# Prompt tokens in groups of 256, 384 and 384, the later ones beside the expert gathers

## The reference

```
xn = rmsnorm(x);  q_lat(384), kv_lat(256), k_rope(32), pool_in(512), gates(2x1024) = xn @ w_in
q = rope(rmsnorm(q_lat) @ w_q_up), 8 heads of 64+32;  c = rmsnorm(kv_lat);  k = [c @ w_uk, rope(k_rope)];  v = c @ w_uv
q and k are RMS-normed per head; prompt: causal softmax over 1024 keys
sample: softmax over 8 x 32 cached pages of 128 tokens (found through page_table) and the 8 new ones
pool: trailing means over 2, 4, 8, 16 tokens minus the token, a linear layer per group
h = x + (sigmoid(g1) * (attn @ w_attn_br) + sigmoid(g2) * (pool @ w_pool_br)) @ w_out
PEER: s = rmsnorm(h) @ w_q scored against 2 x 128 keys, 8 heads; top 16 of each half, top 16 of the 256 sums
      expert ids -> y = h + sum over 8 x 16 experts of softmax gate * gelu(xn2 . u[id]) * v[id]
```

## Time and profile before

| what | value |
|---|---|
| median of 3 runs | 4643.17 us (4634.75 to 4645.33) |
| the profiled execution | 4673.63 us |
| its span, first to last instruction | 4671.8 us |
| mean granted TensorE clock | 0.849 |
| bytes read from and written to HBM | 1275 MB and 29 MB |

### The profile page before, as it was taken

How to read it: one execution, slowest core, us unless ns; L and a number is a source line. 1 busy time by engine, 2 the same in 40 slices (tenths; PEclk the granted TensorE clock), 3 DMA queues, 4 the chain that set the end, 5 groups by cost and what they waited for, 6 DMA issues and landing times.

```text
span 4671.8 us, 47213 instructions
## 1 busy us (share of the span) xinstructions
PE 3692.4 (79%) x13481; PEld 1607.9 (34%) x13481; DVE 2738.3 (59%) x6886; ACT 998.0 (21%) x2045; POOL 2470.3 (53%) x2234
## 2 busy tenths in 40 slices
PE   8998787999998577777877778777878767676556
PEld 4433565444454233333333333333333323230001
DVE  3334331001104878878888888887878765666643
ACT  1121332001200224223323323322322310200000
POOL 0001100000000777777777777777777776677776
PEclk9998878999999788888888888888887878777778
DMA  2002002111323999999999999999999999999999
GB/s 105 1 28 36 2 0 95 41 40 59 109 63 101 361 388 381 396 380 388 396 394 388 388 399 396 392 396 386 396 396 389 374 405 412 386 407 390 372 372 382
DMA packets 441801, 1306.94 MB, mean 280 GB/s; under 512 B 90218, under 2 KB 146923, under 8 KB 438707
## 3 DMA queue, kind: packets, MB, share of 16 engines
q0 software_dynamic: 313344, 1140.99, 62.6%
q1 hardware_dynamic: 128242, 163.51, 10.7%
HBM read 1275.49 MB, written 28.75 MB: 279 GB/s over the span
## 4 chain that ended last, share of the span: by engine, by line
POOL 28%; DMA 14%; PE 11%; issue 10%; DVE 3%; SPq 2%; ACT 1%; DVEq 0%; ACTq 0%; POOLq 0%
POOL arena L1280 28%; DMA arena<-in_peer_v,arena 9%; PE ps_m L1343 4%; PE ps_m L1591 3%; DMA arena<-in_cache_krope 2%; DMA arena<-key_scores 1%; SPq L1544 1%; DMA arena<-in_peer_u,arena 1%; DVE arena L1385 1%; PE ps_m L1581 1%; PE ps_m L1616 1%; PE ps_m L1599 1%; SPq L1542 1%; PE ps_m L1600 1%; PE ps_m L1932 0%
## 5 line engine op out<-in xcount | busy, mean ns | idle before, releaser
L1343 PE MATMUL ps_m<-arena 128*32 128x512 f32 x4352 | 1171.3, 742 | 584.0 <-DMA arena<-in_peer_v,arena 558.3
L1385 DVE CUSTOM_DVE_ANT_0 arena<-arena 128x1024 f32<-128x1024 f32 x1088 | 1318.6, 1225 | 523.1 <-DMA arena<-in_peer_u,arena 491.5
L1280 POOL DMA_INDIRECT arena<-in_peer_u,arena x1088 | 1207.9, 1110 | 639.6 <-issue 329.0
L1280 POOL DMA_INDIRECT arena<-in_peer_v,arena x1088 | 1200.4, 1103 | 403.3 <-issue 306.9
L1343 PEld LDWEIGHTS ps_m<-arena 128*32 128x32 f32 x4352 | 193.8, 120 | 1346.2 <-DMA arena<-in_peer_v,arena 921.5
L1591 PE MATMUL ps_m<-arena 128*128 128x512 f32 x1056 | 567.7, 664 | 2.6 <-ACT arena L1671 2.4
L1581 PE MATMUL ps_m<-const,arena 128*128 128x128 f32 x528 | 135.7, 346 | 177.7 <-DMA arena<-in_cache_krope 148.8
L1591 PEld LDWEIGHTS ps_m<-arena 128*128 128x128 f32 x1056 | 202.5, 213 | 196.9 <-issue 190.5
L1671 ACT ACTIVATE arena<-ps_m 128x512 f32<-128x512 f32 x264 | 158.2, 599 | 514.5 <-PE ps_m L1591 510.0
L944 POOL COPY arena<-arena 128x1024 f32 (+1 forms) x8 | 8.3, 1042 | 489.4 <-POOLq L821 407.4
L1663 ACT ACTIVATE arena<-ps_m 128x256 f32<-128x256 f32 x264 | 101.4, 384 | 689.7 <-PE ps_m L1582 688.7
(11 more groups left out here) (235 smaller groups left out, 4465.4 us busy)
## 6 DMA issues: line engine op xcount, KB each, us to landing
arena<-in_cache_ckv SPq DMA_DIRECT2D x256, 128.0 KB
arena<-in_w_merge SPq DMA_DIRECT2D x16, 1536.0 KB, 9.2
arena<-in_w_peer SPq DMA_DIRECT2D x32, 576.0 KB, 4.1
arena<-in_peer_u,arena POOLq DMA_INDIRECT x1088, 7.6
arena<-in_peer_v,arena POOLq DMA_INDIRECT x1088, 7.6
arena<-key_scores SPq DMA_DIRECT2D x68, 128.0 KB, 10.8
key_scores<-arena SPq DMA_DIRECT2D x32, 256.0 KB, 4.5
arena<-in_w_front SPq DMA_DIRECT2D x1, 4864.0 KB, 18.9
```

The lines of the kernel that those rows point to most:

```text
L1280: self.nc.gpsimd.indirect_dma_start(out=ring[:, slot, :], out_offset=None, in_=self.I[table], in_offset=bass.IndirectOffsetOnAxis(ap=self. ...
L1343: mm = self.nc.tensor.matmul(self.acc[32 * j:32 * j + 32, n, :], self.diag[:, (q0 + j) // 16 % DIAGS, (q0 + j) % 16, :], self.v_ring[:, (q ...
L1385: self.nc.vector.tensor_tensor_reduce(out=u, in0=u, in1=self.xrep[jg % self.XBUF], scale=1.0, scalar=0.0, op0=ALU.mult, op1=ALU.add, accum ...
```

## The change

The front half no longer exists as such. A class `Prompt` with the same arithmetic works on a group of prompt tokens, and there are three: tiles 0 and 1 with the 64 sample tokens (320 columns), tiles 2 to 4, tiles 5 to 7 (384 each). The first is emitted at once on every engine, ahead of the gathers; its first units are routed and its first rows replicated by DMA. The two others are written into the slots of the expert program: `Plan` lays their pieces one behind the other, each with an estimated length in us divided by a rate (2.65 and 2.4 us a slot result), and `paced` raises the rate until the scores are ready before their routing. They take slots 0 to 198 and 199 to 441. The 64 page groups follow at slot 442 with six slots each instead of twelve (842 is their end), the sample's merge, output and scores from 852, four slots a step instead of six.

What comes with it: front, query, merge, output and score weights are loaded once per group, in rings of two or three buffers; keys and values of a group are stored to DRAM and read back with those of the groups before; heads are projected as pairs (128 columns) and the rotary parts as quads; the window sums and the multiply by the norm are on DVE, no longer on POOL; the sigmoid is written as a tanh of the half; the cached latent and rope rows are one tensor, one load a page instead of two; the barrier between the halves is gone.

The diff, cut to its core:

```diff
-PAGES_AT, PAGE_SLOTS = 16, 12
-SAMPLE_AT = PAGES_AT + DB * (NPAGES // GP * PAGE_SLOTS + 2) + 12
+PAGE_SLOTS = 6
...
+GROUPS_OF = (2, 3, 3)
...
+        groups, tile, base = [], 0, None
+        for i, tiles in enumerate(GROUPS_OF):
+            groups.append(paced(i, tile, tiles, base))
+            base, tile = groups[-1].done_at + (2 if i else 0), tile + tiles
+        assert ex.end + GROUP_WORDS <= HALO, (ex.end, HALO)
+        pr = Prompt(env, ex.end, ex.spare, sem, ps, rt, ex, groups)
+        pg = Pages(env, ex.end, sem, ps, base + 8)
...
+            pr.sync(Now(sp), groups[0], groups[1])
+            main = Main("SP", sp, ex.sync(sp))
+            for g, following in zip(groups[1:], after[1:]):
+                pr.sync(main, g, following)
+            pg.sync(main)
+            sm.sync(main)
+            main.finish()
...
+            main = Main("POOL", pool, ex.pool(pool))
+            pg.clear(main, pr)
+            main.finish()
...
+            pr.tensor(Now(pe), groups[0])
+            main = Main("PE", pe, ex.tensor(pe))
+            for g in groups[1:]:
+                pr.tensor(main, g)
+            pg.tensor(main)
+            sm.tensor(main)
+            main.finish()
...
+def route_slot(unit):
+    return TOPK * (unit - 5) + 4
+def paced(i, tile, tiles, base):
+    if base is None:
+        return Group(i, tile, tiles, None, 1.0)
+    rate, unit = 2.4, H * tile
+    while True:
+        g = Group(i, tile, tiles, base, rate)
+        if g.half_at <= route_slot(unit) and g.done_at <= route_slot(unit + 4):
+            return g
+        rate += 0.05
+        assert rate < 20
...
+class Now:
+    def __init__(self, eng):
+        self.eng = eng
+    def to(self, slot):
+        return self.eng
...
+class Plan:
+    def __init__(self, base, rate):
+        self.base, self.t, self.rate, self.begin, self.end = base, base, rate, {}, {}
+    def piece(self, name, us, lead=0):
+        if self.base is None:
+            return
+        self.t += lead
+        self.begin[name] = self.t
+        self.t += us / self.rate
+        self.end[name] = self.t
+    def at(self, name, part=0.0):
+        if self.base is None:
+            return 0
+        return int(self.begin[name] + part * (self.end[name] - self.begin[name]))
...
+class Group:
+    def __init__(self, i, tile0, tiles, base, rate):
+        self.i, self.tile0, self.tiles, self.base = i, tile0, tiles, base
+        self.T, self.first, self.last = tiles * P, i == 0, tile0 + tiles == PT
+        self.N = self.T + (NS if self.first else 0)
+        self.col0 = tile0 * P
+        self.units = [(h, t) for h in range(H) for t in range(tiles)]
+        self.unit0 = H * tile0
+        mm, p = 0.9 * self.N / 512, Plan(base, rate)
+        mt = 0.9 * self.T / 512
+        self.p = p
+        p.piece("sum_x", 8 * mm, 1)
+        for j in range(11):
+            if j == 4:
+                p.piece("sum_q", 3 * mm)
+            if j == 7:
+                p.piece("sum_kv", 2 * mm)
+            p.piece(f"chunk{j}", 8 * mm, 2 if j == 0 else 0)
+        for u in range(6):
+            p.piece(f"q{u}", (4 if u < 4 else 7) * mm, 1 if u == 5 else 0)
+        p.piece("pick_q", mm)
+        for t in range(tiles):
+            p.piece(f"v{t}", 1.8)
+        for s in range(6):
+            p.piece(f"sq{s}", mm, 0.4 if s >= 2 else 0)
+        for u in range(4):
+            p.piece(f"k{u}", 3 * mm, 0.3 if u >= 2 else 0)
+        p.piece("pick_k", 2 * mm, 0.5)
+        for c in range(G):
+            p.piece(f"lin{c}", mm)
+        for s in range(6):
+            p.piece(f"sk{s}", mm, 1 if s == 0 else 0.2 if s >= 2 else 0)
+        for u, (h, t) in enumerate(self.units):
+            n = tile0 + t + 1
+            p.piece(f"a{u}", n * 0.6 + 0.2, 4 if u == 0 else 0)
+        p.piece("a_end", 0.5, 0.5)
+        for t in range(tiles):
+            p.piece(f"at{t}", 1.1, 0.7 if t == 0 else 0)
+        for d in range(KD):
+            p.piece(f"gate{d}", 16 * mt, 1 if d == 0 else 0)
+            p.piece(f"branch{d}", 8 * mt)
+        for k in range(KD):
+            p.piece(f"out{k}", 2 * tiles * 0.9, 1 if k == 0 else 0)
+        for t in range(tiles):
+            p.piece(f"tp{t}", 2.1, 2 if t == 0 else 0.5)
+        for j in range(2 * H):
+            p.piece(f"s{j}", 8 * mt + tiles * 0.25, 0.7 if j == 0 else 0)
+        p.piece("s_end", tiles * 0.25, 0.5)
...
+        self.half_at = 0 if base is None else p.after("s8", 1)
+        self.done_at = 0 if base is None else p.after("s_end", 3)
...
+        for h in range(2, H):
+            u = (h - 1) * g.tiles
+            sp = main.to(g.after(f"a{max(u - 3, 0)}"))
+            sp.wait_ge(self.s_done, g.unit0 + u)
+            self.load_key(sp, g, h)
```

More of the change, by code:

```diff
@@ L123, in build @@
[L123 to L133, removed]
@@ L137 @@
[L137 to L147, removed]
-LATT = ATS - 2 * H * NS
-LATE = LATT - 2 * N_IDS
-QT = TOP - H * TOK
-KT = QT - H * TOK
-CT = KT - 2 * TOK
@@ new lines, in _ @@
+            pr.vector(Now(dve), groups[0])
+            main = Main("DVE", dve, ex.vector(dve))
+            for g in groups[1:]:
+                pr.vector(main, g)
+            pg.vector(main)
+            sm.vector(main)
+            main.finish()
+def route_slot(unit):
[10 more added lines that the diff above has]
+        assert rate < 20
@@ new lines, with __init__, finish, to @@
+class Main:
+    def __init__(self, name, eng, program):
+        self.name, self.eng, self.program, self.at = name, eng, program, 0
+    def to(self, slot):
+        while self.at < slot:
+            next(self.program)
+            self.at += 1
+        return self.eng
+    def finish(self):
+        for _ in self.program:
+            pass
+class Now:
+    def __init__(self, eng):
+        self.eng = eng
+    def to(self, slot):
+        return self.eng
+class Plan:
[12 more added lines that the diff above has]
+        return int(self.begin[name] + part * (self.end[name] - self.begin[name]))
+    def after(self, name, more=0):
+        if self.base is None:
+            return 0
+        return int(self.end[name]) + 1 + more
@@ new lines, in act_scores @@
+    def act_scores(self, main, g):
+        s, ps, i, T = self.nc.scalar, self.ps, g.i, g.T
+        for j in range(2 * H):
+            n = 16 * i + j
+            if g.first and j >= 10 and j % 2 == 0:
+                self.rt.softmax(main.to(0), j // 2 - 5)
+            act = main.to(g.after(f"s{j}") - 1)
+            act.wait_ge(self.q_done, n + 1)
+            if j >= 2:
+                act.wait_ge(self.k_done, n - 1)
+            s.activation(self.qb(g, j % 2), ps[:, 2 + j % 2, 0:T], ACT.Copy).then_inc(self.q_out, 1)
@@ new lines, in dve_scores @@
+    def dve_scores(self, main, g):
+        v, ps, i = self.nc.vector, self.ps, g.i
+        for j in range(2 * H):
+            n, h = 16 * i + j, j // 2
+            if g.first and j >= 10 and j % 2 == 0:
+                self.rt.find(main.to(0), h - 5)
+            dve = main.to(g.after(f"s{j + 1}" if j + 1 < 2 * H else "s_end"))
+            dve.wait_ge(self.k_done, n + 1)
+            if j == 0:
+                dve.wait_ge(self.rows_stored, 32 * (g.tile0 + g.tiles))
+            if j % 2 == 0 and (g.i or h >= 2):
+                dve.wait_ge(self.stored[h % 2], 256 * g.i + 64 * (h // 2))
+            v.tensor_copy(self.score_rows(g, h % 2)[:, :, j % 2, :], ps[:, 4 + j % 2, 0:g.T].rearrange("p (t k) -> p t k", t=g.tiles)).then_inc(self.k_out, 1)
@@ L1798, in vector @@
     def vector(self, main):
-        main.to(PAGES_AT)
+        main.to(self.first)
         self.start_batch()
```

2132 lines of the change are left out of this document (1125 added, 1007 removed).

## The result

The changed kernel took 4722.76 us (median of 4 runs, 4703.13 to 4729.7) against 4644.25 us of the kernel before, measured beside it (4634.75 to 4660.01): a ratio of 1.0159, 95% interval 1.0118 to 1.0200. It is 1.6% slower, where 3955 us and 15% faster were forecast. Its profiled execution took 4723.11 us over a span of 4721.0.

The account below looks back on a forecast made before the run. PE bound the first half, DMA gathers the second; the change lays the first under DMA time. 397 + 677 + 802 + 1320 + 355 + 396 + 30 = 3977 us of span, scaled to 3953; forecast 3955 us, range 3850 to 4100.

Parts of the forecast that it names:

- the one on pages: Slots 442 to 841, six per page group: PE, DMA and DVE nearly equal, plus 0.35 us waiting, 3.3 x 400 = 1320 us.
- The ring: Engines waiting on each other at each page group's end: 4.75 us, up to 7.05 with two dots; 0.35 a slot taken.
- the text on loads: Prompt groups beside the gathers: loads don't stall PE; a 1536 KB weight block landed in 9.5 us, ring slot free some 15.
- the overlap: Page stage: POOL waits only after 8 gathers, some 11 us, so single waits are hidden and only the mean counts.
- The clock: Page stage: if granted clock stays 0.83, PE needs 3.53 us a slot, 1412 us in all; by full clock 1172.
- Head: Everything before the first dot, for 256 prompt and 64 sample tokens: 397 us, range 370 to 440.
- Groups: Prompt groups two and three beside the gathers, slots 0 to 198 and 199 to 441, DMA-bound at 402 GB/s: 677 and 802 us.
- Sample and rest: Sample at slots 842 to 947: 355 us; then 140 slots at 2.83 us: 396 us.
- the clock above 0.9 in the pages: Sign named ahead: PE's granted clock in the page stage would be above 0.9.
- the dip below 390 GB/s: Sign named ahead: DMA rate near 400 GB/s in the groups, dipping below 390 in the pages if the ring costs.
- Starving POOL by DVE: Rival: a DVE near 95% busy makes nearly all gathers wait, 4.54 us a slot, 4970 us in all; chance 0.05.
- the page ring costs its full 4.1 us a slot: Rival: page stage takes 1640 us instead of 1320, since no slot of margin is left; 4270 us in all; chance 0.22.

Follow-up runs that it names:

- the third buffer: Three page buffers in place of two, otherwise the changed kernel: 4305.24 us against 4791.2 with two on chip 9; 0.8954 of the kernel before.
- split loads: Each page's load issued as four DMAs of a quarter of its columns: two page buffers 5239.87 and 5203.24 us, three page buffers 4294.94 us.
- the later chain: Three page buffers, with maxima, exponentials and weighing at a page group's end moved one slot later: 4050.78 us on chip 6, 4176.12 on chip 15.

## Why the prediction was wrong

**The step that failed** is the one on pages: "at each group's end they wait in a ring ... I take 0.35 of waiting: 3.3 x 400 = 1320 us", and with it the upper bound of 4.1 us a slot. The ring held the last key square, root, sums, scaling and maximum. It did not hold the page load, which the text on loads had settled by its landing time under the gathers, for the prompt's weights, and by "a ring slot is free for some 15" us, which is the prompt weights' ring and not the pages'. The page load was thus a wait put at nothing, and it measured 8.3 us in each of 62 groups, 517 us. What was not asked is when the buffer comes free: two buffers, the weighing at slot 5 of a group of 6, the next use at slot 6. The numbers at hand would have bounded it: four issues at up to 0.9 us and a landing of up to 9.5, less the one slot of 3.3, are up to 10 us a group, 640 us in 64; the trace of the changed kernel has 3.67 of issue and 6.1 of landing at the boundary shown. PE stood there for 10.66 us, so nothing of the slot was left as a lead.

With it failed the overlap: "for these POOL waits, but only after 8 gathers, some 11 us ... So single waits are hidden and only the mean counts". The wait for a page and the work around it are longer than the eight buffers cover: at the boundary shown PE forms no v product from 2495.8 to 2518.70, for 22.9 us, and in the whole stage POOL stood 872.9 us for the v products, in 94 waits of up to 19.9 us.

**What the excess consists of**, on chip 6: of the 689 us between 2009 and 1320, 445 went with the third buffer (2009 to 1564, with split loads, whose issuing three buffers hide), 230 with the later chain (1564 to 1334), and 14 are left. On the other chips the two steps are 481 (2020 to 1539, chip 9) and 142 (1549 to 1407, chip 15). The first is the missing term, about 7 us a group. The second is the ring that the prediction did price: 0.35 us a slot were taken and 0.96 were there (with three buffers 1564/400 = 3.91, less the 2.95 taken for the fullest engine). With the chain moved the stage is 1334 us, 3.33 a slot. That this meets the predicted 1320 says nothing for the prediction: it is another kernel, and the 0.38 above 2.95 that are left in it are other waits and what remains of the slow clock; how they share it was not tried.

**The clock.** The prediction weighed it as an aside. In the page stages at hand the granted clock, a mean between 1.2 and 2.4 GHz, was 0.95 with PE busy 90% of the stage, 0.90 at 80%, 0.81 at 66%, 0.76 at 54% (two buffers and split loads: 1313.75 of 2426 us). The matmuls of the keys' product in the same order, PE lines of four kernels (busy, mean ns): the later chain, three buffers with split loads, the changed kernel, two buffers with split loads:

```profile
L1851 PE MATMUL ps<-arena 128*128 128x512 f32 x1052 | 524.7, 622 | 10.4 <-ACT arena L1934 10.0
```

```profile
L1852 PE MATMUL ps<-arena 128*128 128x512 f32 x1044 | 542.5, 644 | 31.7 <-ACT arena L1932 30.9
```

```profile
L1850 PE MATMUL ps<-arena 128*128 128x512 f32 x1052 | 588.0, 687 | 8.9 <-ACT arena L1930 7.9
```

```profile
L1851 PE MATMUL ps<-arena 128*128 128x512 f32 x1044 | 586.3, 690 | 18.0 <-ACT arena L1931 17.0
```

After the wait for a page the first matmuls ran slower: in the timeline above the first pair of L1840 took 0.69 us and the four of L1850 behind it 2.56; from 2520.55 on they took 0.44 and 1.89. So the changed kernel has, beside its longer waits, 124 us more of PE's busy time than the one with the later chain (1322.8 against 1198.9). The Trainium skill (TensorE: Matmul & The Clock Gate, HAM oscillation) has it that a PE stopped again and again for data falls back to the slow clock; the trace agrees by stages and at this boundary.

**The rest of the steps.** Head: 431 against 397, in the range given (370 to 440). Groups: 694 and 834 against 677 and 802; the windows' DMA shares of 0.94 and 0.98 at 360 and 375 GB/s fit DMA as the bound, at less than the 402 taken, though no run tested it. Group two moved 250 MB (360 x 694) where 266 were counted: the v gathers start 20 slots late, so it has 374 gathers and not 398. That made good part of the lower rate. Sample and rest: 346 and 382 against 355 and 396. Of the signs named ahead, the clock above 0.9 in the pages failed (0.82), and the dip below 390 GB/s came, but went to 236; the v gathers did wait for PE. Starving POOL by DVE was hardly put to the test in the changed kernel, whose DVE was busy 56% of the page stage (1117.35 of 2001): its gathers in the page stage of the changed kernel take 1174 and 1059 ns, 1122 and 1095. With the later chain DVE was busy 83% (1106.65 of 1334), and they took 1148 and 1111. The 95% of the rival came in no run. The lines of the changed kernel, both of POOL in 1959:3960:

```profile
L1550 POOL DMA_INDIRECT arena<-in_peer_u,arena x401 | 470.7, 1174 | 122.3 <-issue 122.3
L1550 POOL DMA_INDIRECT arena<-in_peer_v,arena x401 | 424.5, 1059 | 983.5 <-PE ps L1613 872.9 <-issue 110.6
```

The rival "the page ring costs its full 4.1 us a slot" had the right place and half the size (320 of 681 us). The chances gave a slower kernel 0.05, by the wrong mechanism.

Two sums of the prediction are off without bearing on this: the terms of the head add up to 400 us, not 397, and the slot price above which POOL starved would have made the kernel slower is (4671.8 - 397 - 781)/842 = 4.15 us, not 4.27, a mean gather of 1.77 and not 1.83.

**Left open.** The kernel with three buffers and whole loads did not run on chip 6; the one with split loads stands in for it. Why the chain is worth 142 us on chip 15 and 230 to 244 on chip 6 was not tried. With the later chain, the trace from chip 15 has 70 us of PE's waits, at the first transposes of a page and at its keys, for which the profile shows no releaser; the one from chip 6 has next to none of them. Where gathers are slower, part of what the chain frees can only be waiting for DMA (0.91 share at 334 GB/s there against 0.95 at 352), which is argued and not shown.

## What to carry to other kernels

When a loop's period is shortened, write down for each buffer the slot of its last reader, of its next fill and of its next use, and count again: halving a period of 12 slots took this lead from seven to one, not to three and a half, because the last reader stayed at slot 5 of the period that follows. Price the exposed load as issue plus landing less the lead, once a period, and ask whether one more buffer fits: here it turned 0.995 into 0.895 of the time before. Then read the waits again for the chain that the first one covered; moving that by one slot turned 0.896 into 0.870.

## What the runs showed that was not expected

- A kernel that waits more also had PE busy for longer. For the same 5,700 or so matmul records it was busy 1199 us at a granted clock of 0.95 and 1323 to 1327 at 0.81 or 0.82.
- Chips differ, and not evenly between kernels. The kernel before took 4654 us on chip 6 and 4813 to 4856 on four others. Of its two traces the slower moves fewer GB/s under the gathers (366 and 373 against 387 and 394), though POOL's time for a gather is shorter there (1082 and 1088 ns against 1110 and 1103). The changed kernel's ratio was 1.016 on one chip and 0.995 on another, so a ratio from one chip can't be set against a ratio from another to better than 2%.
- At the two boundaries shown an issue on SyncE took 0.71 us for a quarter of a page (11.31/16) and 0.92 for a whole one (3.67/4): a load split in four took three times as long to issue.
